# Moving the rotary swap to DMA, pairing the attention units, and re-ordering a few steps in a two-layer attention and mixture-of-experts trunk

## What is computed

```python
def apply_partial_rope(x, cos, sin):              # ROPE_DIM = 16 of each head's 64
    half = ROPE_DIM // 2
    x1, x2, rest = x[..., :half], x[..., half:ROPE_DIM], x[..., ROPE_DIM:]
    return jnp.concatenate([x1 * c - x2 * s, x2 * c + x1 * s, rest], axis=-1)

def hybrid_mixer(x, ...):
    z = x @ w_in                                   # 1024 -> 6656 columns
    qa, ka, va, ub, qc, kc, vc, ga, gb, gc = jnp.split(z, bounds, axis=-1)
    ya = chunked_relpos_attention(qa, ka, va, rel_bias)
    yb = multiscale_pool_mixer(ub, pool_w, pool_scale)
    yc = differential_attention(qc, kc, vc, lam, ..., cos, sin)   # uses apply_partial_rope
    merged = (sigmoid(ga) * (ya @ w_branch_a) + sigmoid(gb) * (yb @ w_branch_b)
              + sigmoid(gc) * (yc @ w_branch_c))
    return merged @ w_out

x = layer_norm(DN_ALPHA * x + h)
y = shared_expert(xf) + routed_experts(xf)         # 64 experts, top 8
x = layer_norm(DN_ALPHA * x + y)
```

## Time and profile before

| | us |
|---|---|
| median of 3 runs | 1493.58 |
| lowest and highest | 1493.38, 1493.70 |
| the profiled execution, its own time | 1493.22 |
| its span, first to last instruction | 1491.4 |
| PE busy / DVE busy / ACT busy / POOL busy | 1474.6 / 573.3 / 437.3 / 34.6 |
| mean granted TensorE clock | 0.997 |
| moved by DMA, share of the 16 engines in the expert stage | 496 MB, 0.9 and more |

### The profile page before, as it was taken

The page is one execution under the profiler, slowest core; times in us unless marked ns, Lnnn a source line. Parts: engine busy times, 40 slices in busy tenths (PEclk is TensorE's granted clock), DMA queues, the critical chain, the costliest instruction groups (busy, mean ns, idle before and its releaser), DMA issues.

```text
span 1491.4 us, 21154 instructions
## 1 busy us (share of the span) xinstructions
PE 1474.6 (99%) x8738; PEld 937.1 (63%) x8738; DVE 573.3 (38%) x982; ACT 437.3 (29%) x713; POOL 34.6 (2%) x30
## 2 busy tenths in 40 slices
PE   9999999999999999999999999999999999999996
PEld 9999998544444444444399999984444444444442
DVE  4567756321212222221555677671221212222124
ACT  4555544121111111111336544432111111111112
POOL 0111000000000000000001110000000000000000
PEclk9999999999999999999999999999999999999998
DMA  8553459799999999999834344588999999998993
GB/s 310 189 187 128 167 184 409 314 427 424 427 425 427 423 427 424 418 423 425 327 113 170 142 170 170 214 358 352 423 428 423 426 424 426 424 426 358 420 420 142
DMA packets 80074, 496.42 MB, mean 333 GB/s; under 512 B 6128, under 2 KB 11504, under 8 KB 46960
## 3 DMA queue, kind: packets, MB, share of 16 engines
q1 hardware_dynamic: 77696, 491.44, 81.0%
q10 hardware_dynamic: 2288, 3.67, 0.7%
HBM read 494.05 MB, written 1.05 MB: 332 GB/s over the span
## 4 chain that ended last, share of the span: by engine, by line
PE 96%; DVE 3%; ACT 1%; issue 0%; DVEq 0%
PE bank L1680 29%; PE bank L1508 19%; PE bank L1704 15%; PE bank L1633 8%; PE bank L1660 8%; PE bank L1578 5%; PE bank L1463 3%; PE bank L1694 1%; PE bank L1401 1%; PE bank L1425 1%; PE bank L1520 1%; PE bank L1651 1%; PE bank L1642 1%; PE bank L1546 1%; PE bank L1529 1%; PE bank L1432 1%
## 5 line engine op out<-in xcount | busy, mean ns | idle before, releaser
L1508 PE MATMUL bank<-x_hi,w_hi 128*128 128x256 f32 x704 | 202.0, 287 | 0.0
L1508 PE MATMUL bank<-x_hi,w_lo 128*128 128x256 f32 x704 | 199.2, 283 | 0.0
L1508 PE MATMUL bank<-x_lo,w_hi 128*128 128x256 f32 x704 | 199.2, 283 | 0.0
L909 DVE TENSOR_TENSOR w_lo<-ring_w,w_hi 128x2048 fp32r<-128x2048 f32 x71 | 162.3, 2288 | 80.5 <-ACT w_hi L684 80.4
L1319 DVE TENSOR_TENSOR y_lo<-bank,y_hi 128x512 fp32r<-128x512 f32 x128 | 88.5, 692 | 203.2 <-ACT y_hi L826 203.2
L1308 DVE SCALAR_TENSOR_TENSOR hid<-hid,gate_s,bank 128x256 f32<-128x256 f32 x64 | 30.8, 480 | 347.2 <-ACT hid L813 347.2
L826 ACT CAST y_hi<-bank 128x512 fp32r<-128x512 f32 x128 | 75.0, 586 | 255.9 <-PE bank L1704 255.9
L684 ACT CAST w_hi<-ring_w 128x2048 fp32r<-128x2048 f32 x71 | 135.1, 1904 | 50.8 <-PE bank L1578 28.8
L813 ACT ACTIVATE hid<-bank 128x256 f32<-128x256 f32 x64 | 24.6, 384 | 402.3 <-PE bank L1680 402.3
L1508 PEld LDWEIGHTS bank<-x_hi,w_hi 128*128 128x128 f32 x704 | 135.0, 192 | 4.0 <-issue 2.7
L1508 PEld LDWEIGHTS bank<-x_lo,w_hi 128*128 128x128 f32 x704 | 135.0, 192 | 0.1
(11 more groups left out here) (229 smaller groups left out, 2046.6 us busy)
## 6 DMA issues: line engine op xcount, KB each, us to landing
arena<-in_expert_w_gate_up SPq DMA_DIRECT2D x24, 4096.0 KB, 18.3
gu_a<-in_expert_w_gate_up SPq DMA_DIRECT2D x24, 4096.0 KB, 17.3
ring_w<-in_expert_w_gate_up SPq DMA_DIRECT2D x32, 2048.0 KB, 15.1
ring_w<-in_w_in SPq DMA_DIRECT2D x25, 2048.0 KB, 8.6
arena<-in_expert_w_down SPq DMA_DIRECT2D x24, 2048.0 KB, 16.2
dn_a<-in_expert_w_down SPq DMA_DIRECT2D x24, 2048.0 KB, 16.1
dn_c<-in_expert_w_down SPq DMA_DIRECT2D x16, 2048.0 KB, 15.0
ring_w<-in_w_out SPq DMA_DIRECT2D x4, 2048.0 KB, 8.4
```

Source lines behind the costliest of these rows:

```text
L909: v.tensor_tensor(chunk_part(w_lo, n), chunk_in(n), chunk_part(w_hi, n).bitcast(F32), ALU.subtract).then_inc(w_lo_ready, 1)
L1508: ins = mm(b[:, S * c:S * c + S], lhs, rhs, start=(k == 0 and a + w == 0), stop=(k == KD - 1 and a == 1))
```

## The change

Six edits. They remove, move and add work; the engines' streams are otherwise as before.

1. **Rotary swap by transfers.** The `rope` tasks and the constant `rotate` go; the sign moves into the `sin` table. SP copies rows of qc (after block 6 is issued) and kc (after block 7) within SBUF into `pooled`, five DMAs each, and DVE makes the rotation in three operations on 80 partitions x 1024 for each of the two.
2. **Units in pairs.** `scores`, `turn` and `pv` of two units stand together after z 6, 8, 10, 12, 14, 16 and 17, instead of one unit's after each z from 5 to 17. `probs_t` has two buffers.
3. **Turns ahead of the late gather**, in the first pair of a layer only.
4. **Fewer opening matmuls and constants**: four and four `keep_warm` instead of six and six, 64 KB less in `load_consts`.
5. **Last combine by token tile**: the first half of the columns finishes token tile 0 before tile 1, and DVE adds the residual of that quarter between the two `y_lo` of the last pair.
6. **Third `w_lo` chunk of layer 1** made one pair later on DVE.

```diff
-for _name, _width in (("ident", P), ("cos", S), ("sin", S), ("rotate", P), ("mask", S), ("iota", SLOTS),
+for _name, _width in (("ident", P), ("cos", S), ("sin", S), ("mask", S), ("iota", SLOTS),
...
-        5: sc(0), 6: sc(1), 7: tr(0) + sc(2), 8: [("pv", 0, 0)] + tr(1) + sc(3),
-        9: [("pv", 1, 0)] + tr(2) + [("rope", 0, 0), ("rope", 0, 1)],
-        10: [("pv", 2, 0)] + tr(3) + [("rope", 1, 0), ("rope", 1, 1)],
-        11: [("pv", 3, 0)] + sc(4), 12: sc(5), 13: tr(4) + sc(6),
-        14: [("pv", 4, 0)] + tr(5) + sc(7), 15: [("pv", 5, 0)] + tr(6), 16: [("pv", 6, 0)] + tr(7),
-        17: [("pv", 7, 0)] + [("branch", 0, j) for j in range(4)], 18: [("pool", 0, 0), ("pool", 1, 0)],
+        6: sc(0) + sc(1), 8: tr(0) + tr(1) + sc(2) + sc(3),
+        10: [("pv", 0, 0), ("pv", 1, 0)] + tr(2) + tr(3),
+        12: [("pv", 2, 0), ("pv", 3, 0)] + sc(4) + sc(5), 14: tr(4) + tr(5) + sc(6) + sc(7),
+        16: [("pv", 4, 0), ("pv", 5, 0)] + tr(6) + tr(7),
+        17: [("pv", 6, 0), ("pv", 7, 0)] + [("branch", 0, j) for j in range(4)], 18: [("pool", 0, 0), ("pool", 1, 0)],
...
-        probs_t = view(9216, 4, 2, P)
+        probs_t = [view(9216, 4, 2, P), view(18432, 4, 2, P)]
...
+            def swap_halves(l, i):
+
+                src = (qc_t, kc_t)[i]
+                for h in range(2):
+                    wait_evac(sp, l, ("z", (6, 8)[i] + h, 0))
+                if i:
+                    sp.wait_ge(rope_ready, 2 * l + 1)
+                half = ROPE_DIM // 2
+                for dst_row, src_row, rows in ((0, half, half), (half, 0, half), (ROPE_DIM, ROPE_DIM, CHUNK - ROPE_DIM),
+                                               (CHUNK, CHUNK + half, half), (CHUNK + half, CHUNK, half)):
+                    sp.dma_start(pooled[dst_row:dst_row + rows], src[src_row:src_row + rows]).then_inc(swapped_in, 16)
...
                 for n in range(0 if l == 0 else 2, NB - 2):
                     load_block(l, n)
+                    if n in (6, 7):
+                        swap_halves(l, n - 6)
...
-                    if l == 0 and task == ("z", 9, 0):
+                    if l == 0 and task == ("z", 11, 0):
...
+            def residual(l, which, t, h):
+
+                dve.wait_ge(acc_done if which else h_ready, 2 * TT * l + TT * h + t + 1)
+                part = x_tok[:, t, 512 * h:512 * h + 512]
+                step(v.scalar_tensor_tensor(out=part, in0=part, scalar=ALPHA, in1=acc[t][h][:],
+                                            op0=ALU.mult, op1=ALU.add))
...
-                    k = 2 * l + which
...
-                            dve.wait_ge(acc_done, 2 * TT * l + TT * h + t + 1)
                         part = x_tok[:, t, 512 * h:512 * h + 512]
-                        step(v.scalar_tensor_tensor(out=part, in0=part, scalar=ALPHA, in1=acc[t][h][:],
-                                                    op0=ALU.mult, op1=ALU.add))
+                        if not (which == 1 and t == h == 0):
+                            residual(l, which, t, h)
                         settle()
                         step(v.bn_stats(stats[:, h, :], part))
...
+            def rope(l, i):
+
+                dve.wait_ge(swapped_in, 16 * 5 * (2 * l + i + 1))
+                raw, swapped = (qc_t, kc_t)[i][0:ROPE_ROWS], pooled[0:ROPE_ROWS]
+                sin, cos = [const(name)[0:ROPE_ROWS].unsqueeze(1).to_broadcast([ROPE_ROWS, KW, S]) for name in ("sin", "cos")]
+                step(v.tensor_tensor(swapped, swapped, sin, ALU.mult))
+                step(v.tensor_tensor(raw, raw, cos, ALU.mult))
+                settle()
+                v.tensor_tensor(raw, raw, swapped, ALU.add).then_inc(rope_ready, 1)
...
-                dve.wait_ge(rope_ready, 4 * (l + 1))
+                dve.wait_ge(rope_ready, 2 * (l + 1))
...
-                    elif kind == "rope":
...
-                        free(v.tensor_tensor(turned, pair, const("sin").unsqueeze(1).to_broadcast([P, 2, S]), ALU.mult),
-                             l, task)
-                        step(v.tensor_tensor(plain, raw, const("cos").unsqueeze(1).to_broadcast([P, 2, S]), ALU.mult))
...
-                        v.tensor_tensor(raw, plain, turned, ALU.add).then_inc(rope_ready, 1)
...
+                    if task == ("z", 10, 0):
+                        rope(l, 0)
+                    if task == ("turn", 3, 1):
+                        rope(l, 1)
...
                     v.tensor_scalar(onehot_t[:], const("tokens"), token_s[:, step:step + 1], None, ALU.is_equal).then_inc(onehot_t_ready, 1)
+                    if last and l + 1 < L:
+                        split_low(l + 1, 2)
                     for h in range(2):
+                        if last and h == 1:
+                            residual(l, 1, 0, 0)
                         dve.wait_ge(y_hi_ready, 2 * n + h + 1)
                         part = slice(512 * h, 512 * h + 512)
                         v.tensor_tensor(y_lo[:, part], (bank_other, bank_up)[h][:], y_hi[:, part].bitcast(F32),
...
-                    pair_step(n, double(start - HALVES, l, 3, 1), u, u, n - l)
+                    pair_step(n, double(start - HALVES, l, 3, 1), u, u, n - l, last=u == 1)
                     if u == 0 and l + 1 < L:
-                        for c in range(WBUFS):
+                        for c in range(2):
...
-                            keep_warm(b, 6, hid[:, 0:P], hid[:])
...
-                            keep_warm(b, 6, hid[:, 0:P], hid[:])
...
-                            pe.wait_ge(rope_ready, 4 * (l + 1))
+                            pe.wait_ge(rope_ready, 2 * (l + 1))
...
-                                ins = mm(o, val, probs_t[:, m, kt, :], start=(kt == 0), stop=(kt == qt))
-                    elif kind == "rope":
-                        wait_evac(pe, l, ("z", (6, 8)[i] + j, 0))
-                        if l == 0:
-                            pe.wait_ge(const_in, 32)
-                        for c in range(2):
-                            ins = mm(b[:, S * c:S * c + S], const("rotate"), (qc_t, kc_t)[i][:, 2 * j + c, :],
-                                     start=True, stop=True)
+                                ins = mm(o, val, probs_t[i % 2][:, m, kt, :], start=(kt == 0), stop=(kt == qt))
...
@@ -1687,13 +1701,16 @@
                         pe.wait_ge(y_ready, 2 * n)
                         pe.wait_ge(onehot_t_ready, n)
                         combine(0)
-                    for q in late:
-                        gather(following, q)
+                        for q in late:
+                            gather(following, q)
                     pe.wait_ge(hid_ready, n + 1)
                     for k in range(KF):
                         ins = nc.tensor.transpose(bank_up[:, P * k:P * k + P], hid[:, k::KF], ident)
                     ins.then_inc(hid_turned, 1)
-                    if not first:
+                    if first:
+                        for q in late:
+                            gather(following, q)
+                    else:
                         combine(1).then_inc(combined, 1)
                     pe.wait_ge(hid_t_ready, n + 1)
                     pe.wait_ge(dn_in[slot], 16 * loads)
...
                 pe.wait_ge(onehot_t_ready, 2 * start)
-                for half in range(2):
-                    for part, ready, count in ((y_hi, y_hi_ready, 4 * start - 1 + half), (y_lo, y_ready, 4 * start - 1 + half)):
-                        pe.wait_ge(ready, count)
-                        for t in range(TT):
-                            ins = mm(acc[t][half][:], onehot_t[:, P * t:P * t + P], part[:, 512 * half:512 * half + 512],
-                                     start=False, stop=True, skip_group_check=True)
-                            if part is y_lo:
-                                ins.then_inc(acc_done, 1)
+                pe.wait_ge(y_ready, 4 * start - 1)
+                for t in range(TT):
+                    for part in (y_hi, y_lo):
+                        ins = mm(acc[t][0][:], onehot_t[:, P * t:P * t + P], part[:, 0:512],
+                                 start=False, stop=True, skip_group_check=True)
+                    ins.then_inc(acc_done, 1)
+                for part, ready in ((y_hi, y_hi_ready), (y_lo, y_ready)):
+                    pe.wait_ge(ready, 4 * start)
+                    for t in range(TT):
+                        ins = mm(acc[t][1][:], onehot_t[:, P * t:P * t + P], part[:, 512:1024],
+                                 start=False, stop=True, skip_group_check=True)
+                        if part is y_lo:
+                            ins.then_inc(acc_done, 1)
...
+            sin[base + n] = -np.sin(ang[:, n])
```

26 lines of the change are left out of this document (8 added, 18 removed).

## The result

| | before | changed |
|---|---|---|
| median | 1493.64 | 1482.85 |
| lowest and highest of four runs | 1493.38, 1494.18 | 1482.37, 1482.95 |
| ratio of the medians, 95% interval | | 0.9927 (0.9914 to 0.9939) |
| span of the profiled execution | 1491.4 | 1481.0 |
| PE busy | 1474.6 | 1463.1 |

A forecast was written before the change was run, and what follows sets the result against it. PE was taken to bound the kernel, busy 1474.6 of 1491.4 us. Terms summed to 10.15 us, taking 1493.22 to 1483.1 profiled, 1483.4 for the median; range 1481.3 to 1487.4, holding the forecast (1481.9 to 1485.3) and Rival A.

The forecast's parts named there:

- Rope off PE: Mixer: removing two rope visits of PE in each of two layers gains 1.70 us each, 6.8 us (6.6 to 7.0).
- Visits: Mixer: six fewer PE visits to the attention per layer, at 0.13 us each, gain 1.6 us (1.0 to 2.3).
- The slack under it: Softmax of units 6 and 7: margin 0.1 to minus 0.7 us, booked loss 0.4 us in all (0 to 3).
- Rival A: Mixer: pairs run late at units 6 and 7, or a bank at z 9; +2 to +4 us per layer pair total, chance 0.13.
- The copies: Rotary swap: qc and kc copies within SBUF land in time at the lower transfer price; cost 0 us (0 to 8).
- B: Rival: kc's copies land late at the upper price, PE waits 4 us per layer; +8 us, 1491.4, chance 0.04.
- D: Rival, slower: kc's copies land more than 99.5 us into the run; landing at 101 gives 1500.0 us, chance 0.03.
- Turns ahead of the gather: First pair of each layer: turns before the late gather gain 0.65 us a layer, 1.3 us.
- Third `w_lo`: End of layer 0: DVE free sooner, so PE's turns follow the combine sooner; 0.55 us once (0.4 to 0.6).
- Last combine: End of each layer: residual before the second y_lo saves a DVE pause; 0.15 us per layer, 0.3 in all.
- Opening: Start to z 2: four fewer keep_warm gain 0 us (0 to 0.3), since PE waits for block 1.
- Rival C: Opening: with four keep_warm PE's clock stays low through z 0 and z 1; +9.5 us, 1492.9, chance 0.04.

The follow-up runs named there:

- e1_single: The changed kernel with one unit's scores, turns and pv after each z from 5 to 17 again, swap by transfers kept; median 1490.82 us.
- e6_pool_more: The changed kernel with one more POOL operation in unit 7, between scaling and subtraction; median 1484.46 us.
- e5_swap_slow: The changed kernel with kc's third and fifth copies issued only after those before them have landed; median 1486.77 us.
- e12_before_again: The kernel before the change, unaltered, run and profiled a second time; median 1493.52 us.
- e7_combine_old: The changed kernel with the last combine in its old order and no residual between the two y_lo; median 1482.39 us.
- e4_warm0: The changed kernel without the eight opening matmuls on zeros (0 and 0 instead of 4 and 4); median 1482.95 us.
- e10_changed_again: The changed kernel, unaltered, run and profiled again; median 1483.39 us.
- e11_warm6: The changed kernel with six and six opening matmuls on zeros instead of four and four; median 1482.67 us.
- e2_ln_late: The changed kernel with ACT's 1 MB layer norm load issued behind the last-but-one pair's two y_hi instead of ahead; median 1481.67 us.
- e3_first_undone: The changed kernel with the first pair of a layer in the old order, late gathers ahead of the turns; median 1483.51 us.

## Why the prediction was right, point by point

**What bounds the kernel.** PE, as it said, and work taken from PE counted in full in the mixer. The rule's condition, that nothing else becomes late, failed at one place, and not in the mixer stage. The sign by which the forecast was to be wrong did not come: PE's busy time fell by 11.5 us, and its idle time grew by 1.1 and not by more than 2.

**Rope off PE, 6.8 us.** Right. The excursions after z 9 and z 10 shrank by 1.72 in each layer (e1_single), 6.9 in all. The rows of before were enough for this term.

**Visits, 1.6 us (1.0 to 2.3).** The mechanism was right, the size was off by more than the bounds. The two mixers gained 10.41, less 6.9 for the rope: 3.5 us, or 0.29 for a visit. e1_single gives 1.90 for six, 0.32, with a restart of some 0.1 to 0.2 behind its wait in it. The step that failed is the reading of the price: 0.09 on the way in plus 0.10 on the way out left out what lies inside the scores' own 0.66 us. Sixteen small matmuls take 1.20 us from the first to the next product (52.21 to 53.41), and eight take 0.66, so eight more cost 0.54 and 0.12 of every visit are turn-over; this is read from two counts and adds up with the other two to 0.31. Rival E, that fewer visits save nothing, did not come. And "visits that end in turns pay perhaps half" had no row behind it; it took the 0.19 down to 0.13, when the true value was above.

**The slack under it, a loss of 0.4.** The margin of 0.1 to minus 0.7 was worked out, and it is 0.1 (trace and e6_pool_more). No loss. The better end came true because DVE had nothing else to do: unit 7's subtraction took 1.28 us, with DVE idle between 121 and 124.3, and not the 2.16 of the earlier trace rows. Rival A's argument (POOL suffers beside DVE) had no occasion to show, and it had misread a row: the 1.29 at 116.13 also stood beside DVE, which read a bank from 116.56 on. The 2.16 stood beside this operation of DVE, which reads `arena` twice:

```profile
123.31 1.50 DVE L998 TENSOR_TENSOR arena<-arena 128x1020 f32<-128x1020 f32 x1
```

The other half of A, a bank that comes back late at z 9, did come in part, in layer 0 only. The 0.2 us of margin hang on the opening: there is no wait where z 2 starts at 23.07 or later, and 0.26 to 0.75 us in the six profiles of paired units with the old order on ACT in which it starts at 22.82 or sooner. What an early opening gains is mostly lost there.

**The copies, cost 0 (0 to 8).** Right, with the lower price. Issues take 0.65 instead of 0.5 us, and the rotation starts at 90.0 instead of 89. The slack of "over 3 us" is 2.5. e1_single and e5_swap_slow show that B's mechanism exists: with some 4 us less cover than here PE waits 1.0 to 2.0 us there. Nothing came near D's landing at 99.5 or later.

**Turns ahead of the gather, 1.3 us.** Right in the place, and 1.5 in size (0.75 and 0.76). But 0.64 of layer 0's share was taken back.

**Third `w_lo`, 0.55.** 0.43 (0.46 by the turns, which follow the combine by 0.34 and not by the 0.25 foreseen). Against e12_before_again, where PE came later and its wait for `hid` was shorter, it is 0.25. No run undoes this edit alone.

**Last combine, 0.3.** Nothing: e7_combine_old. The working had called it "at about the same moment", and it starts 0.06 us behind; the pause of 0.1 that it was to save is worth 0.03.

**Opening, 0.** No effect of the edit (e4_warm0, e10_changed_again, e11_warm6). The 0.75 us of the profiled execution fit the spread that these profiles show. The sum had treated the opening of one execution as fixed, when it moves by 0.25 us between two profiles of the kernel before, by 0.4 between two of the changed one, and by 1.4 over all its versions. Rival C's mechanism is real, as e4_warm0 shows; at four and four it reached the transposes of x in some executions, and not the products.

**Not in the sum: the last load of layer 0, minus 1.05.** The page said a DMA share of 0.9 and more in the expert stage, and the table by stretches would have said 1.01. Before the change the load had landed at 725.75, with PE asking at 726.13. That margin of 0.4 us behind a stage of full DMA is the row that the prediction did not look for, and the 0.75 us of the first pair stand inside that stage. Taken from the first pair of layer 0, they are more than the margin; the rest of the 1.05 is the landing, which was 0.6 us later in this profile and 0.4 in the second one of the kernel before. The 5.2 us of the mixer have no part in it, since e1_single waits 0.71 us with none of them in layer 0. e2_ln_late and e3_first_undone show both halves: less to carry brings 0.75 us back, and the old order of the first pair makes the wait shorter by 0.65.

So the terms that were too small (1.9 for the visits, 0.2 for the first pairs, 0.4 for the loss that did not come) and those that were too large or missing (1.05, 0.75, 0.4 for the combine, 0.1) nearly cancel. That the total was met so closely, 1482.85 for the 1483.4 that was said, is luck; that it lies in the range is owed to the rope and the visits.

## What to carry to other kernels

Price a change of work on a pipelined engine from two rows with different counts, not from the gaps at the ends of one: the turn-over hides inside the small group's own length. Where a second resource runs at a full share for hundreds of microseconds, work saved on the first inside that stage counts only up to the margin with which the stage's last transfer lands, while work saved ahead of the stage counts in full. So read this margin first, and move transfers that nobody waits for yet out of its way. Keep one execution's opening apart from the rest when two versions are compared; here it moves by over 1 us between versions whose opening is the same or nearly so, and a few tight places further on give part of it back.
